# One of four token tiles of a product-key expert layer moves from dense matmuls to gathered rows

## The reference, cut to what matters

```
e = i1 * N_KEYS + i2                       # t x 8 heads x 16 picks, of 16384 experts
g = softmax(c_top)
act = gelu(einsum('thkd,td->thk', u[e], x))
y = einsum('thk,thkd->td', g * act, v[e])
```

## Time and profile before

| | |
|---|---|
| median of 3 executions | 2347.56 us |
| profiled execution, span from first to last instruction | 2350.9 us |
| PE busy | 2288.5 us, 97% |
| DVE, ACT, POOL busy | 57%, 39%, 50% |
| granted TensorE clock, mean | 0.992 |
| chain that ended last | PE 56%, no other above 2% |
| HBM read, written | 286.06 MB, 72.37 MB |

### The profile page before, as it was taken

One profiled execution on the slowest core, in us unless ns is written; L12 is line 12 of the kernel. 1 busy time (PEld: TensorE's weight loads), 2 busy tenths in 40 slices (PEclk: granted clock), 3 DMA queues, 4 the chain that ended last, 5 costly groups with the idle time before them and its releaser, 6 DMA issues.

```text
span 2350.9 us, 29628 instructions
## 1 busy us (share of the span) xinstructions
PE 2288.5 (97%) x11229; PEld 1143.2 (49%) x11429; DVE 1347.7 (57%) x2765; ACT 915.8 (39%) x1095; POOL 1178.3 (50%) x558
## 2 busy tenths in 40 slices
PE   8999999999999999999999999999999999999998
PEld 4556444444444564544566444444444444444443
DVE  3668474554425545898896555555555544555555
ACT  3233342333333443111687333344444334444432
POOL 1002346655543347410000676666666666888873
PEclk9999999999999999999999999999999999999999
DMA  6031358989752239834588886666666666776641
GB/s 220 0 108 37 142 168 247 259 238 262 226 156 72 72 126 261 223 117 157 206 323 311 286 244 201 197 197 192 192 194 189 193 170 176 200 203 172 173 113 45
DMA packets 404136, 427.16 MB, mean 182 GB/s; under 512 B 276258, under 2 KB 343078, under 8 KB 392500
## 3 DMA queue, kind: packets, MB, share of 16 engines
q1 hardware_dynamic: 397684, 414.05, 58.3%
q10 hardware_dynamic: 6336, 11.54, 1.3%
HBM read 286.06 MB, written 72.37 MB: 152 GB/s over the span
## 4 chain that ended last, share of the span: by engine, by line
PE 56%; DMA 2%; POOL 1%; ACT 1%; issue 1%; DVE 1%; SPq 1%; POOLq 0%; ACTq 0%; DVEq 0%
PE ps L1860 27%; PE ps L2168 23%; PE ps L2207 3%; DMA gate_matrix<-split 1%; PE ps L2184 1%; PE ps L2185 1%; DMA ring<-in_peer_v 1%; SPq L691 1%; PE ps L2133 1%; ACT split L1382 1%; POOL u_split L955 0%; POOL split L836 0%; PE ps L2073 0%; DMA arena<-u_split 0%; POOL u_split L841 0%
## 5 line engine op out<-in xcount | busy, mean ns | idle before, releaser
L1860 PE MATMUL ps<-split,arena 128*128 128x512 bf16 x3712 | 819.7, 380 | 5.8 <-DVE consts L2940 1.6
L1860 PEld LDWEIGHTS ps<-split,arena 128*128 128x128 bf16 x3792 | 371.1, 98 | 449.5 <-issue 4.3
L2168 PE MATMUL ps<-arena 128*128 128x512 bf16 x1886 | 415.7, 379 | 2.1 <-DMA arena<-u_split 0.3
L961 POOL TENSOR_TENSOR split<-ring,split 128x1024 bf16<-128x1024 f32 x140 | 299.3, 2146 | 76.4 <-ACT split L1417 76.4
L836 POOL TENSOR_TENSOR split<-ring,split 128x4096 bf16<-128x4096 f32 x26 | 207.2, 7971 | 197.1 <-ACT split L1189 194.7
L1860 PE MATMUL ps<-arena,split 128*128 128x512 bf16 x1316 | 296.8, 381 | 5.0 <-DVE arena L2640 2.0
L2168 PEld LDWEIGHTS ps<-arena 128*128 128x128 bf16 x1920 | 187.7, 98 | 227.2 <-DMA arena<-u_split 0.8
L955 POOL TENSOR_TENSOR u_split<-ring,u_split 128x1024 bf16<-128x1024 f32 x80 | 167.7, 2127 | 191.1 <-ACT u_split L1404 191.1
L947 POOL TENSOR_TENSOR split<-ring,split 128x1024 bf16<-128x1024 f32 x44 | 92.7, 2138 | 258.1 <-ACT split L1414 258.1
L1860 PEld LDWEIGHTS ps<-arena,split 128*128 128x128 bf16 x1344 | 142.9, 107 | 150.0 <-DVE arena L2640 6.1
L1417 ACT ACTIVATE split<-ring 128x1024 bf16<-128x1024 f32 x140 | 146.3, 1054 | 172.2 <-POOL ring L971 66.6
(11 more groups left out here) (357 smaller groups left out, 3125.1 us busy)
## 6 DMA issues: line engine op xcount, KB each, us to landing
ring<-in_peer_v SPq DMA_DIRECT2D x32, 2048.0 KB, 8.3
ring<-in_peer_u SPq DMA_DIRECT2D x20, 2048.0 KB, 12.0
ring<-in_w_ff SPq DMA_DIRECT2D x16, 2048.0 KB, 8.2
gate_matrix<-split SPq DMA_DIRECT2D x16, 2048.0 KB, 7.5
arena<-gate_matrix SPq DMA_DIRECT2D x32, 1024.0 KB, 6.8
arena<-in_peer_u SPq DMA_DIRECT2D x48, 512.0 KB, 4.8
turned_table<-u_split SPq DMA_DIRECT2D x48, 512.0 KB, 5.6
ring<-turned_table SPq DMA_DIRECT2D x12, 2048.0 KB, 9.1
```

Source lines behind the costliest of these rows:

```text
L961: pool.tensor_tensor(part_place(i, 1), block, part_place(i, 0), ALU.subtract).then_inc(v_lo, 1)
L1860: mm = pe.matmul(dst, a(k), b(k), start=n == 0, stop=n == len(terms) - 1)
L2168: mm = pe.matmul(up_bank(j), a, b, start=n == 0, stop=n == len(terms) - 1)
```

## The change

The tokens are in four tiles of 128. Tiles 1 to 3 (384 tokens, `TD`) stay dense; every up matmul has 384 columns now, and gate blocks, gate matrix and stored gelu results are three quarters of their size. The down product is a plain three-pass product for all 32 groups, 72 matmuls of 512 columns each (3 token tiles, 2 halves of the width, 4 expert tiles, 3 passes). Its six outputs stay in PSUM banks 0 to 5 over all groups and are added to x once at the end, so DVE adds no outputs on the way. The live up tiles have banks 6 and 7 only.

Tile 0 is computed from its picked rows. For each of its 128 pick slots (8 heads x 16) POOL issues an indirect DMA that brings each partition (token) the 1024-wide u row that it picked, 512 KB in all; DVE multiplies it with x and sums it into `dots`. After 128 of them ACT takes gelu, DVE multiplies by the gates, and 128 more gathers bring the v rows, which DVE adds to x with a per-token factor. There are four row buffers; POOL may be four rows ahead. DVE takes 6 rows during selection, 24 during the gates, 14 in each pair round, 8 in each single round.

There are 14 early groups in place of 11, so 14 pair rounds and 4 singles; 30 early tiles in the selection, 24 in the gates. DVE does half of the low parts of u (`u_low`); POOL does the low parts of v and the gathers.

```diff
+TD = T - P
+PICKS = P_HEADS * TOPK
...
-        SELECTED, GATED, EARLY, PRE = 25, 16, 11, 12
+        SELECTED, GATED, EARLY = 30, 24, 14
+        LIVE = EX_GROUPS - EARLY
+        PRE = EARLY
...
+        def up_bank(j):
+            return bank(6 + j % 2)[:, 0:TD]
+        def down_bank(t, c):
+            return bank(2 * (t - 1) + c)
...
+            for p in range(24, 2 * PRE):
+                pre_pair(p, p < 2 * PRE - 1)
+                slot_free(p - 24)
+                load_turned(p - 20)
...
+            slot_free(12)
+            load_v(0)
+            sp.wait_ge(gate_out, TD // HB + 2)
+            for half in range(2):
+                turn_rows(EARLY, half)
             load_gelu(0)
...
+                sp.wait_ge(u_lo, 4 * i + 4)
+                load_u(g + 2)
+                sp.wait_ge(ex_a, 4 * g + 2)
+                turn_rows(g + 1, 0)
+                sp.wait_ge(v_lo, 4 * (s + 1) + 4)
+                load_v(s + 3)
                 sp.wait_ge(ex_a, 4 * g + 4)
+                turn_rows(g + 1, 1)
+                sp.wait_ge(live_mul, 4 * i + 4)
+                load_gates(s + 3)
...
+            for p in range(24, 27):
+                pre_late(p)
             pool.wait_ge(key_tops, 2 * P_HEADS)
-            for t in range(NT):
-                sums(t)
+            sums(0)
+            sums(1)
+            pre_late(27)
+            sums(2)
+            sums(3)
...
+            def gather(n):
+                b, uses = row_place(n)
+                table, k = (ins["peer_u_2"], n) if n < PICKS else (ins["peer_v_2"], n - PICKS)
+                if uses >= 1:
+                    pool.wait_ge(rows_taken, row_before(n) + 1)
+                pool.indirect_dma_start(row_buf[:, b, :], None, table[0],
+                                        bass.IndirectOffsetOnAxis(row_index[:, k:k + 1], 0)).then_inc(row_in[b], 16)
...
+            gathers(27, 34)
+            for j in range(4):
+                v_low(0, j)
+            n = 34
             for i in range(EARLY):
+                for m in range(8):
+                    v_low(2 * i + 1 + m // 4, m % 4)
+                    more = (1, 2)[m % 4 < 3]
+                    gathers(n, n + more)
+                    n += more
...
+            def down_tile(s, t, c, j):
+                rows_, cols = slice((t - 1) * P, t * P), slice(j * D + c * 512, j * D + (c + 1) * 512)
+                hi, lo, wh, wl = act_hi[s % 2][:, j, rows_], act_lo[s % 2][:, j, rows_], split[:, s % 2, 0, cols], split[:, s % 2, 1, cols]
+                for n, (a, b) in enumerate(((hi, wh), (hi, wl), (lo, wh))):
+                    mm = pe.matmul(down_bank(t, c), a, b, start=s == 0 and j == 0 and n == 0, stop=s == EX_GROUPS - 1 and j == 3 and n == 2)
+                return mm
...
+                live_tile(g, 0)
+                live_tile(g, 1)
...
+                down(2 * i)
+                live_tile(g, 2)
+                live_tile(g, 3)
+                down(2 * i + 1)
...
+            def row_taken(n):
+                b, uses = row_place(n)
+                dve.wait_ge(row_in[b], 16 * (uses + 1))
+                if n < PICKS:
+                    dve.scalar_tensor_tensor(row_buf[:, b, :], row_buf[:, b, :], 1.0, x_row, ALU.mult, ALU.mult,
+                                             accum_out=dots[:, n:n + 1]).then_inc(rows_taken, 1)
+                else:
+                    dve.wait_ge(rows_taken, n)
+                    dve.scalar_tensor_tensor(x_sb[:, 0, :], row_buf[:, b, :], dots[:, n - PICKS:n - PICKS + 1], x_sb[:, 0, :],
+                                             ALU.mult, ALU.add).then_inc(rows_taken, 1)
...
+                rows_taken_to(n, n + 1)
+                live_low(g, s, 0)
+                live_times(g, s, 1)
+                rows_taken_to(n + 1, n + 2)
+                live_low(g, s, 1)
```

More of the change, by code:

```diff
@@ new lines, in gathers, with v_low @@
+            def gathers(first, last):
+                for n in range(first, min(last, 2 * PICKS)):
+                    gather(n)
+            def v_low(s, j):
+                pool.wait_ge(v_hi, 4 * s + j + 1)
+                at = slice(j * D, (j + 1) * D)
+                pool.tensor_tensor(split[:, s % 2, 1, at], ring[:, s % 2, at], split[:, s % 2, 0, at], ALU.subtract).then_inc(v_lo, 1)
+            pool.wait_ge(index_ready, 1)
+            pool.wait_ge(pre_lo, 4 * PRE)
+            gathers(0, 6)
@@ L1012, in _ @@
+            for s in range(2 * EARLY + 1, EX_GROUPS):
+                for j in range(4):
+                    v_low(s, j)
+                    gathers(n, n + 2)
+                    n += 2
+            gathers(n, 2 * PICKS)
             for t in range(NT):
@@ L1581, in _ @@
+            act.wait_ge(rows_taken, 2 * PICKS)
+            act.wait_ge(live_lo, 4 * LIVE)
+            sum_squares(x_sb[:, 0, :], ps[:, 6:8, :].rearrange("p a b -> p (a b)"), 0)
+            for t in range(1, NT):
+                act.wait_ge(mm_out, MM["last"] + 2 * t)
                 sum_squares(x_sb[:, t, :], ps[:, 6:8, :].rearrange("p a b -> p (a b)"), t)
@@ new lines, in hidden_here, with down @@
+            def hidden_here(s, j):
+                pe.wait_ge(v_lo, 4 * s + j + 1)
+                if s < 2 * EARLY and s % 2 == 0:
+                    pe.wait_ge(stored_lo, 2 * s + j + 1)
+                else:
+                    pe.wait_ge(live_lo, 4 * (down_group(s) - EARLY) + j + 1)
+            def down(s):
+                for j in range(4):
+                    hidden_here(s, j)
+                    for t in range(1, NT):
+                        for c in range(2):
+                            mm = down_tile(s, t, c, j)
+                mm.then_inc(downs, 1)
@@ L2909, in _ @@
             numbers = iota2.unsqueeze(1).to_broadcast(four)
-            for k in range(T // HT):
+            for k in range(TD // HT):
                     def by_token(row):
@@ new lines, in _, with add_last @@
+            for s in range(2 * EARLY, EX_GROUPS):
+                for j in range(4):
+                    live_times(s, s, j)
+                    rows_taken_to(n, n + 1)
+                    live_low(s, s, j)
+                    rows_taken_to(n + 1, n + 2)
+                    n += 2
+                    if j >= 2:
+                        u_low(s + 1, j)
+                u_low(s + 2, 0)
+                u_low(s + 2, 1)
+            def add_last(t, c):
+                dve.wait_ge(mm_done, MM["last"] + 2 * (t - 1) + c + 1)
```

879 lines of the change are left out of this document (336 added, 543 removed).

## The result

The changed kernel takes 2569.87 us (median of 5, 2552.45 to 2601.82) where the kernel before takes 2348.8. The ratio is 1.0918, 95% interval 1.0883 to 1.0954, without the slowest execution, 2601.82, which lies over 1.5% above the fastest. The forecast was 2200, and its range ended at 2330. The profiled execution has a span of 2600.0 us and lies some 30 us above the median.

What follows compares the result with a forecast made beforehand. The prediction took the DMA engines to become the bound in the pairs: PE's floor of 2101 plus 14 x 6.8 and 4 x 1.9 gave a span of 2204, less 3.3 for the median, so 2200 us, range 2095 to 2330.

Steps and rivals of the forecast that it cites:

- The early part: Selection and gates: picks ready at 1139, PE waiting some 23 us, gates ending at 1289, first down product at about 1323.
- the lockstep rival: Pairs and singles: DVE and POOL hinder each other, round 59 us, single 36, time 2290; chance 0.12.
- PE: Pairs and singles: matmul work of 46.7 us a pair round and 31.1 a single.
- VectorE and POOL: Pair round: DVE busy 32 of 46.7 us, POOL's v low parts 16.9 us plus 14 gather issues; neither binds.
- the rival on the slower side: POOL's gather issue, taken as 1.5 us: from 3.3 us as slow as before, at 4 us 2505; chance 0.12.
- Starved gates: Gates: DVE's bfloat16 operations keep POOL from writing gather descriptors; 2330 us, likelier 2245; chance 0.08.
- The DMA engines in a round: Pair round: 30 to 37 us of loads and transposes plus 17.2 of gathers, 48 to 54 together, 53.5 taken.
- streams wait for each other: Pair round: reason for taking 53.5 us, near the upper end of the 48 to 54 us of DMA need.
- The pessimistic bound: Pair round: gathers only at the transposes' 203 GB/s take 2.6 us each, round 66 to 73 us; no chance given.
- 2101: Whole span: floor in us from the first down product at 1323 plus 777.7 of PE work and tail.
- The single round's sum: Single rounds, DMA engines: 0.60 x 39 less 1, plus 8 gathers at 1.23 us, is 32.5; 33 taken.
- The latency of a gather: Skill's rule: 3.2 us for 512 KB; four in flight allow a row each 0.8 us and leave the sum unchanged.

Runs made afterwards that it cites:

- e6: e1 and e4 together: changed kernel without gathers, u's high and low parts for the group after next at the round's end; 2127.3 us.
- e16: e12 with plain copies of the same bytes in place of the live groups' transposes; 2133.6 us.
- e1: Changed kernel with all 256 gathers left out, VectorE doing its row operations on x instead; 2179.88 us.
- e12: e10 and e4 together: all gathers run unread, u's parts for the group after next at the round's end; 2365.2 us.
- e10: Changed kernel with all gathers running, but VectorE not waiting for them and working on a row that lies ready; 2562.4 us.
- e4: Changed kernel with u's high and low parts for the group after next moved from mid-round to the round's end; 2413 and 2510 us.
- e11: Changed kernel with 7 rows, not 11, ahead of live tile 2, and stored tiles and u's parts behind live tile 3; 2388.2 us.
- e13: e11 with no row between VectorE's product with a live tile and its low part; 2417 to 2485 us.
- e14: e13 with the load of u behind the round's first two transposes in SyncE's queue; 2443 to 2528 us.
- e15: e11 with 50 rows taken beside the gates in place of 24, and 12 in a pair round in place of 14; 2373 to 2430 us.
- e3: Changed kernel with each gather replaced by a direct DMA from POOL's queue of 128 consecutive rows; 2535.2 us.
- e8: e4 with POOL waiting for the live group's transposes before certain gathers, to keep the two kinds apart; 2570.8 us.

## Why the prediction was wrong

**The early part: right in kind, 9 us short.** PE takes the first picks at 1140.04 and the last at 1146.23 (forecast 1139), is done with the gates at 1299.25 (1289), and starts the first down product at 1332.33 (1323). PE stood idle before 1140 for 9.6 + 15.6 us, forecast 23. The gates began 7 us later than forecast, at 1149.02. A step took 5.69 us on VectorE, forecast 5.84, but four of the last five took 7.6 to 8.6. In each of them one of VectorE's bfloat16 operations took 3.15 us in place of 1.22, while POOL did a low part of u:

```profile
1253.47 2.29 POOL L959 TENSOR_TENSOR u_split<-ring,u_split 128x1024 bf16<-128x1024 f32 x1 [5.72 <-ACT u_split L1357]
...
1253.68 3.17 DVE L2834 TENSOR_TENSOR arena<-arena 128x2048 bf16<-128x2048 bf16 x1
```

That is the hindrance of the lockstep rival, and here it cost some 8 us.

**PE: right.** 46.7 us a round in e6, to the tenth.

**VectorE and POOL: near enough.** A row is 1.30 us (u) and 1.45 (v), a low part of u 1.46 on VectorE where 1.2 was taken, and VectorE is busy 35 us of a round, forecast 32. A gather issue takes 1.31 and 1.19 on POOL against the 1.5 taken. POOL is busy 42%; the rival on the slower side, 3.3 us an issue, is refuted. So is the lockstep as the cause: e16 keeps VectorE's rows and POOL's gathers and has rounds of 48.1.

**Starved gates: refuted.** Between VectorE's bfloat16 operations POOL issued a gather every 5.69 us in 1.68 us. The rule of the Trainium skill (SBUF — State Buffer, SBUF: two separate sides) is visible at most in those 1.68 us: the issue at 1294.67, when VectorE had finished its last row, took 0.94. What cost VectorE time in the gates was POOL's own work on SBUF, as above, not the gathers.

**The DMA engines in a round: here it failed.** "I take 53.5, near the upper end, since the streams wait for each other in program order." The sum was 37 for loads and transposes and 14 x 1.23 = 17.2 for gathers. Measured in the changed kernel: 10.67 MB a round (84.68 MB in 400/50.4 rounds of e1) x 4.42 = 47.2, and 14 x 2.17 = 30.4, together 77.6 us. That this is the round of 78.9 at a share of 0.99 proves nothing by itself, as the prices are made from the same share; what it shows is how they divide. The 37 was right for a round without gathers (e1: 10.67 x 3.48 = 37.1) and 17.2 nearly right for gathers without transposes (e16: 14 x 1.38 = 19.3). Wrong was to add them: side by side each makes the other dearer. With the order out of the way they need the 63.9 us of e12, 10.4 more than the 53.5; in the changed kernel the other 15 us come from the order and from rows that are waited for. The pessimistic bound, 2.6 us a gather and a round of 66 to 73, was nearer and came from the nearest row: 203 GB/s while transposes run. It was given no rival and no chance, although 2101 + 14 x 19.3 = 2371 is already slower than the kernel before. So the only slower case in the forecast was POOL's, which did not come, and the range ended below this bound. The single round's sum, 32.5, is 32.2 by its own terms; that changes nothing.

**The order: missed.** That u's parts for the group after next wait for transposes of the same round, ahead of the live tile on VectorE, stood in the code and in no step of the forecast. It was priced as "streams wait for each other", 0 to 6 us. It is worth 53 us alone (e1 against e6) and 197 when transposes are late (e10 against e12). So each fault makes the other worse.

Laid end to end, one path of several: 2127 without gathers and with the later order; +6 with gathers, and copies in place of the transposes (e16); +232 with the transposes back (e12), of which about half is what the plain sum of the two would cost; +48 to 145 when VectorE must wait for the rows (e4); the rest up to 2570 for the order. The forecast of 2200 held 73 us above e6 for everything behind the first number. By the times of PE, from one first down product to the next: 13 rounds at 77.4 in place of 53.5 are 311 us. The stretch behind them, to the first single's down product, holds six live tiles and took 90.1 in place of 63.2, 27 more. Three singles at 49.6 in place of 33 are another 50, the start 9. That is 397 on 2204, 2601, against the span of 2600.0.

The latency of a gather from the Trainium skill (DMA: Bandwidth & Descriptors, Anatomy of one DMA), 3.2 us for 512 KB by its rule, was set aside in the forecast as without effect. The chain above shows 11.85 us. By the page's figure four buffers would give a row every 0.8 us, by the trace's one every 3 us; both are estimates.

Not settled: why a 256-byte transpose packet and a 4 KB gather packet hinder each other; no run changes the size of either packet alone. Nor is it settled how much of the loss lies on the engines and how much in SyncE's full queue. Nor was a kernel found that beats both: e11 stays 1.7% above the kernel before, and what lies below is bought with work left out.

## What to carry to other kernels

Before adding transfers to a loop that already holds DMA transposes, price both kinds at the rate of the stretch where the transposes run, not at that of plain loads, and do not add shares that were measured apart. Then walk each engine's instruction order once with every transfer late, since an operation for the round after next that waits for this round's transfer holds back what the matmuls need now. Look, too, at how long the issuing queue is held. And test with transfers that nobody reads: they separate load from latency, once the order is out of the way (e10 alone showed nothing, e12 did).

## What the runs showed of the hardware beyond that

- A DMA share of 1.00 does not say that the engines are at their end. e16 moves 375 GB/s at 1.00 and TensorE is hardly kept waiting; the changed kernel moves 230 at 0.99, e12 280 at 1.10.
- Beside plain transfers gathers are cheap. e16 with 134 MB of them is 6 us above e6, whose live groups are turned and not copied. Beside the gate stores of the changed kernel (1160 to 1280) one costs the engines 0.215 x 120 / 9.59 x 0.524 = 1.41 us:

```profile
q1 hardware_dynamic: 2160, 31.46, 63.8%
q0 software_dynamic: 2628, 9.59, 21.5%
```

- Some of these kernels do not repeat: e4, e13, e14 and e15 spread over 57 to 97 us between executions, the kernel before over 6. It does not go by the transfers alone: e3, e8 and e12, with both kinds in full, spread over 5.
- A wait of 2.05 us on PE was followed by matmuls at a lower granted clock, 0.51 to 0.63 for some 4 us: 9.62 us for what takes 7.93 (e1).
- Beside gathers a transpose holds the queue that issues it: 13.5 us in the median in e12, 2.5 in e6.
